# One plain fp32 matmul in place of three rounded ones in the mixers of a two-layer diffusion backbone

## What is computed

```python
hc = ctx * (1 + mods_c[1]) + mods_c[0]
proj_c = hc @ (w_in[l][:, :SCAN_COLS] if last else w_in[l])
xh_c, b_c, c_c, dtf_c, dtb_c = ssd_prepare(proj_c[..., :SCAN_COLS], conv_w[l], conv_b[l])
...
h = x * (1 + sc1) + sh1
proj = h @ w_in[l]
...
merged = (jax.nn.sigmoid(proj[..., COL_GP:COL_GS]) * y_pool
          + jax.nn.sigmoid(proj[..., COL_GS:W_IN_COLS]) * y_s)   # y_s = normed y @ w_ssd_out
return merged @ w_o
...
x = layer_norm(DEEPNORM_ALPHA * x + g1 * mix, ln_g[l, 0], ln_b[l, 0])
```

## Time and profile before

| | us |
|---|---|
| median of 3 runs | 4869.28 (4862.14 to 4878.07) |
| the profiled execution (its span) | 4879.2 |
| context projection, at 44 to 161 | 117 |
| context merge, at 269 to 413 | 144 |
| latent finish, at 1432 to 1556 | 124 |
| latent projection, at 2984 to 3151 | 167 |
| latent merge, at 3260 to 3508 | 248 |

### The profile page before, as it was taken

One profiled execution on the slowest core, in us unless ns is written; L12 is line 12 of the kernel. 1 busy time (PEld: TensorE's weight loads), 2 busy tenths in 40 slices (PEclk: granted clock), 3 DMA queues, 4 the chain that ended last, 5 costly groups with the idle time before them and its releaser, 6 DMA issues. The chain is left out here.

```text
span 4879.2 us, 47619 instructions
## 1 busy us (share of the span) xinstructions
PE 3455.5 (71%) x15218; PEld 1732.2 (36%) x15218; DVE 3203.2 (66%) x6594; ACT 1529.7 (31%) x3727; POOL 2178.8 (45%) x1603
## 2 busy tenths in 40 slices
PE   7788888987768987555555557979897555555555
PEld 5576323432357433111111115767742111111111
DVE  5365787664465668776776756674566677677775
ACT  2452344343262225222222223372222222222221
POOL 3253444443022454555555552323245555555554
PEclk9889999998879999767777778979999777777777
DMA  4536999999732999999999992232299999999998
GB/s 180 212 126 226 390 419 407 413 425 376 293 126 91 375 419 394 406 416 417 408 422 419 413 424 79 71 104 78 87 373 405 421 406 421 417 416 423 413 420 356
DMA packets 263605, 1596.67 MB, mean 327 GB/s; under 512 B 43885, under 2 KB 50861, under 8 KB 77357
## 3 DMA queue, kind: packets, MB, share of 16 engines
q0 software_dynamic: 184320, 1342.26, 66.5%
q1 hardware_dynamic: 77738, 248.58, 14.0%
q10 hardware_dynamic: 1296, 2.79, 0.2%
HBM read 1575.86 MB, written 17.66 MB: 327 GB/s over the span
## 5 line engine op out<-in xcount | busy, mean ns | idle before, releaser
L2465 PE MATMUL banks<-arena 128*64 128x512 f32 x5120 | 1596.4, 761 | 1106.6 <-ACT arena L2288 1102.8
L2072 POOL DMA_INDIRECT arena<-in_experts,arena x1280 | 1524.1, 1191 | 1615.7 <-PE banks L2465 1350.6
L2158 DVE CUSTOM_DVE_ANT_0 arena<-arena,token_copies 128x1024 f32<-128x1024 f32 x1280 | 1625.5, 1288 | 686.0 <-DMA arena<-in_experts,arena 618.9
L2465 PEld LDWEIGHTS banks<-arena 128*64 128x64 f32 x5120 | 387.0, 167 | 2154.1 <-ACT arena L2288 1517.0
L2281 ACT ACTIVATE arena<-arena 128x2 f32<-128x2 f32 x640 | 131.2, 205 | 1768.3 <-DVE arena L2158 1754.8
L286 POOL TENSOR_TENSOR wide_low<-wide_blocks,wide_high 128x1024 fp32r<-128x1024 f32 x136 | 340.6, 2526 | 594.9 <-ACT wide_high L276 594.9
L2288 ACT ACTIVATE arena<-arena 128x64 f32<-128x64 f32 x1280 | 376.2, 340 | 293.3 <-POOL arena L1943 251.9
L2344 PE MATMUL banks<-arena,wide_blocks 128*128 128x512 f32 (+3 forms) x960 | 311.5, 474 | 8.4 <-ACT arena L2187 6.7
L324 PE MATMUL banks<-activation_a,wide_high 128*128 128x512 f32 (+1 forms) x768 | 277.8, 362 | 8.5 <-ACT arena L348 2.7
L2417 PE MATMUL banks<-arena,wide_blocks 128*128 128x512 f32 x576 | 276.9, 618 | 0.0
L326 PE MATMUL banks<-activation_a,wide_low 128*128 128x512 f32 (+1 forms) x768 | 269.2, 351 | 0.0
(11 more groups left out here) (256 smaller groups left out, 4679.3 us busy)
## 6 DMA issues: line engine op xcount, KB each, us to landing
wide_blocks<-in_wide SPq DMA_DIRECT2D x168, 1024.0 KB
arena<-cum_rows SPq DMA_DIRECT2D x80, 256.0 KB, 3.2
arena<-in_experts,arena POOLq DMA_INDIRECT x1280
pre_scan<-arena SPq DMA_DIRECT2D x16, 256.0 KB
arena<-pre_scan SPq DMA_DIRECT2D x16, 256.0 KB, 9.1
residual<-in_tokens SPq DMA_DIRECT2D x6, 512.0 KB
arena<-mod_rows SPq DMA_DIRECT2D x6, 512.0 KB
norm_rows<-in_keys SPq DMA_DIRECT2D x3, 1024.0 KB
```

The lines of the kernel that those rows point to most:

```text
L2072: pool.indirect_dma_start(out=v.ring[:, g % RING], out_offset=None, in_=io["experts"], in_offset=bass.IndirectOffsetOnAxis(ap=c.idx[:, u % ...
L2158: last = nc.vector.tensor_tensor_reduce(out=u_row, in0=u_row, in1=k.copies[:, n % NJ], scale=1.0, scalar=0.0, op0=ALU.mult, op1=ALU.add, a ...
L2465: mm = nc.tensor.matmul(k.ps[j * QUAD:(j + 1) * QUAD, a + half], v.lhs[:, g % 4, j], v.ring[:, (g * NJ + j) % RING, D + half * BANK:D + (h ...
```

## The change

In the five stages `product` does one fp32 matmul per pair of tiles, on the weight block as it landed and on the activation as fp32. The splitting goes on all engines: `round_wides`, `cut_wides`, `take_wide` and `modulate_rest` are gone, the second writing of modulated tiles, the second half of the dt matmuls, and the splits of y and of the merged sum. TensorE waits for a block's landing in place of its split. In `stage_project` the turned tiles are copied by ScalarE instead of VectorE, and the scan products rotate over four banks instead of two. In `stage_merge` the pooling products move to banks 2 and 3.

```diff
-def round_wides(k, act, last):
-    while k.next_round <= last:
...
-        for rows in HALVES:
-            k.nc.scalar.copy(k.wide_hi[:, n % HI_SLOTS, rows], k.wide[:, n % WIDE_SLOTS, rows]) \
-                .then_inc(k.wide_rounded.sem, 1)
...
-def cut_wides(k, pool, last):
...
-            k.nc.gpsimd.tensor_tensor(k.wide_lo[:, n % WIDE_SLOTS, rows], k.wide[:, n % WIDE_SLOTS, rows],
-                                      k.wide_hi[:, n % HI_SLOTS, rows].bitcast(F32), ALU.subtract) \
-                .then_inc(k.wide_cut.sem, 1)
...
+def wait_wide(k, pe, n):
+
+    pe.wait_ge(k.wide_landed[n % WIDE_SLOTS].sem, 16 * (n // WIDE_SLOTS + 1))
...
 def product(k, pe, out, lhs, rhs, ready=None):
...
-        if kt == KT // 2 and k.second_half:
-            pe.wait_ge(k.wide_cut.sem, k.second_half)
-            k.second_half = 0
-        (lh, ll), (rh, rl) = lhs(kt), rhs(kt)
-        signal_used(k, nc.tensor.matmul(out, lh, rh, start=(kt == 0), stop=False))
-        nc.tensor.matmul(out, lh, rl, start=False, stop=False)
-        last = nc.tensor.matmul(out, ll, rh, start=False, stop=(kt == KT - 1))
+        last = k.nc.tensor.matmul(out, lhs(kt), rhs(kt), start=(kt == 0), stop=(kt == KT - 1))
+        if kt == 0:
+            signal_used(k, last)
...
-        if kt >= 2:
-            act.wait_ge(k.h_ready.sem, k.h_ready.at(kt - 1))
-        for dst, sig in ((k.act_a[:, kt, 0:T], None), (v.hraw[:, kt % 2, 0:T], k.h_hi)):
...
+        k.nc.scalar.activation(k.act_h[:, kt, 0:T], k.ps[:, kt % 2, 0:T], ACT.Identity,
+                               bias=v.modc[:, 0, kt:kt + 1], scale=v.modc[:, 1, kt:kt + 1]).then_inc(k.h_ready.sem, 1)
...
-            for n in range(2 * KT):
-                kt, q = n % KT, n % 4
...
+            for kt in range(KT):
+                q = kt % 4
...
+            def copy_turned(act, m):
+
+                act.wait_ge(k.turned.sem, k.turned.at(m + 1))
...
+                if 3 <= m < 3 + X_TILES + B_TILES:
+                    copy_turned(act, m - 3)
```

The stages' own lines change in the same way, for instance in the output products of `stage_merge` and `stage_finish`:

```diff
+                if n == 1:
+                    pe.wait_ge(k.merged1.sem, k.merged1.at(KT))
                 if n >= 4:
                     pe.wait_ge(k.mix_read.sem, k.mix_read.at(n - 3))
 
                 product(k, pe, k.ps[:, n % 4, 0:WIDE], lambda kt: mT(kt, slice(t * P, (t + 1) * P)),
-                        lambda kt: tuple(part[:, kt] for part in w),
-                        ready=(lambda kt: pe.wait_ge(k.merged_lo.sem, k.merged_lo.at(kt + 1))) if n == 0 else None) \
+                        lambda kt: w[:, kt],
+                        ready=(lambda kt: pe.wait_ge(k.merged1.sem, k.merged1.at(kt + 1))) if n == 0 else None) \
```

More of the change, by code:

```diff
@@ L28 @@
 U32 = mybir.dt.uint32
-F32R = mybir.dt.float32r
 ALU = mybir.AluOpType
@@ L113, in sb, with alias @@
         return nc.alloc_sbuf_tensor_at(name, shape, dt, offset=k.place[name])
-    def alias(name, shape, other, words=0, dt=F32R):
+    def alias(name, shape, other, words=0, dt=F32):
         return nc.alloc_sbuf_tensor_at(name, shape, dt, offset=k.place[other] + 4 * words)
@@ L120, in setup @@
     k.wide = sb("wide_blocks", [P, WIDE_SLOTS, KT, WIDE])
[L121 to L126, removed]
+    k.copies = sb("token_copies", [P, NJ, D])
+    k.rows = sb("norm_rows", [P, 2, D])
+    k.gates = alias("pooled_gates", [P, 8, SEQ], "token_copies")
     k.ident = sb("identity", [P, P])
@@ L138, in setup @@
     split = lambda name, at: alias(name, [P, KT, SEQ], "arena", at)[:]
[L139 to L143, removed]
+    k.act_h = split("modulated", A_HT)
+    k.act_y = split("gated_outputs", A_XTOK)
     k.ps = ctx.enter_context(nc.psum_tensor("banks", [P, 8, BANK], F32))
@@ L505, in more_mods @@
         x.advance(16 * rounds)
-    k.cut0, k.next_round, k.next_cut = k.cut0 + count, k.next_round + count, k.next_cut + count
     return m
@@ L545, in stage_project @@
     n_wide = 12 if full else 8
-    last_cut = n_wide - 1 if layer == 0 else n_wide
-    hT = lambda kt, cut=slice(0, T): (k.act_a[:, kt, cut], k.act_d[:, kt, cut])
+    hT = lambda kt, cut=slice(0, T): k.act_h[:, kt, cut]
     ld = k.loaded.base
@@ L600, in _ @@
             pe.wait_ge(k.loaded.sem, ld + 48)
-            for n in range(2 * KT):
-                kt, q = n % KT, n % 4
-                last = nc.tensor.matmul(k.ps[32 * q:32 * q + 32, 6, 0:T], v.wdt[:, kt], hT(kt)[n // KT].bitcast(F32),
-                                        start=(n < 4), stop=(n >= 2 * KT - 4))
+            for kt in range(KT):
+                q = kt % 4
+                last = nc.tensor.matmul(k.ps[32 * q:32 * q + 32, 6, 0:T], v.wdt[:, kt], hT(kt),
+                                        start=(kt < 4), stop=(kt >= 4))
             last.then_inc(k.dt_parts.sem, 1)
             for n in range(zg):
-                wh, wl = take_wide(k, pe, w0 + 8 + n // NT)
-                if n == 2:
-                    pe.wait_ge(k.padded.sem, k.padded.at(SCAN_TILES))
+                w = k.wide[:, (w0 + 8 + n // NT) % WIDE_SLOTS]
+                t = n % NT
+                if t == 0:
+                    wait_wide(k, pe, w0 + 8 + n // NT)
+                if n < 2:
+                    pe.wait_ge(k.padded.sem, k.padded.at(SCAN_TILES - 1 + n))
                 if n >= 4:
                     pe.wait_ge(k.z_done.sem, k.z_done.at(n - 3))
-                t = n % NT
                 product(k, pe, k.ps[:, n % 4, 0:WIDE], lambda kt: hT(kt, slice(t * P, (t + 1) * P)),
-                        lambda kt: (wh[:, kt], wl[:, kt])).then_inc(k.z_proj.sem, 1)
+                        lambda kt: w[:, kt]).then_inc(k.z_proj.sem, 1)
                 if n == 2:
@@ L651, in _ @@
             for n in range(zg):
-                if n % NT == 0 and n >= NT:
-                    round_wides(k, act, w0 + min(8 + n // NT + 1, last_cut))
                 act.wait_ge(k.z_proj.sem, k.z_proj.at(n + 1))
@@ L664, in _ @@
                     decay.decays(act)
-        @block.gpsimd
-        def _(pool):
-            cut_wides(k, pool, w0 + last_cut)
         @block.vector
@@ L709, in stage_project @@
     k.consts_set.advance(2)
-    for s in (k.xt_ready, k.h_hi, k.h_ready):
+    for s in (k.xt_ready, k.h_ready):
         s.advance(KT)
@@ L1781, in stage_finish @@
     k.rms_ready.advance(1)
-    for x in (k.ys_proj, k.merged1, k.yt_turned, k.yt_copied, k.y_hi, k.merged_hi, k.merged_lo):
+    for x in (k.ys_proj, k.merged1, k.yt_turned, k.yt_copied):
         x.advance(8)
```

188 lines of the change are left out of this document (51 added, 137 removed).

## The result

The changed kernel takes 4917.1 us at the median (4911.4 to 4922.9, 4 runs), the kernel before 4868.2 in the same session (4862.1 to 4878.1, 4 runs). The ratio is 1.0097, with a 95% interval of 1.0079 to 1.0114: slower by 1.0%, 49 us. Forecast was +74, 4943, in a range from 4910 to 4985. The time lies in the range, close to its lower end, and the +49 just under the "slower by 50 to 100 us" that had been given 0.80. The sign and the mechanism held; of the forecast 74 us a third did not come.

The account below looks back on a forecast made before the run. TensorE was taken to set four of five stages, VectorE, held up by GpSimd's splitting, the context projection. Stage nets 37 + 26 + 13 + 10 - 12 gave +74 (141 growth, 67 returned) on 4869.28: 4943, range 4910 to 4985.

Parts of the forecast that it names:

- growth: Five stages: longer plain fp32 products on TensorE's path add 141 us, 17 of it in the context projection.
- relief: Five stages: splitting work and waits that go away return 67 us, uncertain by 20 either way.
- The price, 512 columns: Eight-step product in the stages: two records of 0.430 us per plain matmul, 6.88 us against 5.57, +1.31.
- The rival built on the ratio 4/3, 4994: Five stages: four passes against three make products a third longer, 192 us less 67, +125; chance 0.05.
- The price, 256 columns: Eight-step product in the stages: two records of 0.224 us per plain matmul, 3.58 us against 2.87, +0.71.
- Tails: Ends of latent merge and latent finish: 1.6 and 1.9 us added, in the merge because the fourth layer norm comes late.
- about 3 us in all: Latent merge start: turned tiles written once save a ScalarE pass each, but four transposes then set the pace.
- a rival in the wrong direction: Six kinds of section: one more product each at 1.2 GHz, twice as long, 41 us more, 4984; chance 0.04.
- The context projection: TensorE becomes the bound, 3.58 us a product; the stage ends at 149 instead of 161, net -12, the only gain.
- what would show it: Right: 2560 product records, sigmoids 6.9 us apart, taps 2.16 us, no TensorE wait for VectorE, latent merge about 285 us.
- the signs of being wrong: Fewer or closer records, shorter stages outside the context projection, granted clock under 1.00 in dense stretches, or waits for weight blocks.

Follow-up runs that it names:

- price-alone kernel: Kernel before with one plain fp32 matmul per product step instead of three split ones, all splitting work and waits kept: 4978.2 us, ratio 1.0221.

## Why the prediction was nearly right

By stage, in us: growth and relief as forecast, and as measured (growth is the price-alone kernel less the kernel before, relief the changed kernel less the price-alone kernel).

| stage | forecast growth, relief, net | measured growth, relief, net |
|---|---|---|
| latent merge | 46, -9, +37 | 44.7, -15.6, +29.0 |
| latent projection | 32, -6, +26 | 29.0, -6.5, +22.6 |
| latent finish | 20, -7, +13 | 17.0, -7.8, +9.1 |
| context merge | 25, -15, +10 | 17.6, -14.1, +3.5 |
| context projection | 17, -29, -12 | 0.1, -14.0, -13.9 |
| sum | 141, -67, +74 | 108.3, -58.0, +50.3 |

**The price, 512 columns.** +1.31 forecast, 6.86 - 5.57 = +1.29 measured. Right, and with it the reading that a plain matmul leaves two records. A product's time grew by a factor of 1.23, not 4/3: a split matmul takes 0.23 us, more than a quarter of a plain one's 0.86. The rival built on the ratio 4/3, 4994, is out. By the Trainium skill ("FP8 and Floating Point Precision", section "TensorE Precision Notes") true FP32 takes four passes; counted against three single ones they do not give the time here.

**The price, 256 columns.** This is the term that was mis-sized. I took 0.224 a record, "nearer the middle of its bounds"; it is 3.46 / 16 = 0.216, half of 512's as the lower bound had it. The growth is 0.59 and not 0.71 a product. That is 0.12 for each of 73 products outside the context projection, 9 us. The lower bound was half of the measured price for 512; the upper one, 3.72 / 16, held the last matmul's tail, which a dense run pays once and not sixteen times. The middle between them had no claim.

**Tails.** I added 1.6 and 1.9 us at the ends of the latent merge and finish. In the merge the read of the product that completes the first row tile stands at 3515.71 and the last operation ends at 3540.42: 24.7 us, where it had been 24.3. TensorE's later products let the first three norms move under them, and the fourth was no later.

```profile
3515.71 0.42 DVE L1267 TENSOR_TENSOR arena<-banks,arena 128x256 f32<-128x256 f32 x1 [2.16 <-PE banks L277]
...
3539.14 1.28 DVE L1023 SCALAR_TENSOR_TENSOR residual<-residual,arena 128x1024 f32<-128x1024 f32 x1
```

With 1.29 and 0.59 the four stages outside the context projection would grow by 110 us (52 products of 512 and 73 of 256), and they grew by 108.3. Two of them differ from it by more than their spread. The latent merge grew by 44.7 and not 42.6: the price-alone kernel's first product takes 10.2 us at a granted clock of 0.69, that of the kernel before 7.2 at 0.85, so that it costs 3.0 more where a product at full clock costs 1.29. The context merge grew by 17.6 and not 20.7: TensorE waited there four times, 2.6 us in all, for the rest of a split block from GpSimd (L286), and in the price-alone kernel, where products are longer, not once.

**Relief.** Right in three stages to within a microsecond, though in the latent projection its spread of 4.0 between profiles is larger than that. In the latent merge I had 9 and it is 15.6: at the start I counted a ScalarE pass a tile with the transposes next in line, "about 3 us in all", and it is 8.5. Of that, 5.4 are the turning, and 3.1 the first product, which had not been counted at all: it now starts at full clock. Nearly 2 of the 3.1 only undo the extra growth named above; against the kernel before, the first product is done 5.5 us earlier (19.7 and 14.2). I had seen that the latent stages start at the lower level and used it only for a rival in the wrong direction.

**The context projection.** TensorE did become the bound, at 3.67 us a tile, and the stage ends 103 us after its start (100 and 101 in the two profiles without the fall of the clock); I had 105. Growth and relief do not add up here: taken first, the price costs nothing, since VectorE sets the scan (117.0 and 117.1), and the relief without the price is 26.3. With both, the price costs 12.4 (90.8 to 103.2, or 9.5 with the stage at 100.3), where 24 x 0.59 = 14 would be the whole of it. That GpSimd held up VectorE is shown twice, by taking its work away and by putting it back.

Of the 24 us between +74 and +50, 15 are growth outside this stage (9 the 256-column price, 3 the tails, 3 the waits in the context merge), 6 relief (the latent merge's start), 2 this stage.

**What stood under "what would show it".** The 2560 records of `product`, 16 between two sigmoids that stand 6.9 us apart (6.86), taps of 2.16 and no wait of TensorE for VectorE in the scan came as written; the latent merge is 277 and not 285 long; the three lookups are as long as before within 4 us. Of the signs of being wrong one did appear in small: the granted clock is under 1.00 in two dense stretches, 0.83 at the end of the context projection (1.7 us) and 0.91 from 3120 to 3140 in the latent projection. The kernel before has 0.91 in the same place of its latent projection (3114 to 3134), so at least that one is no effect of plain matmuls.

## What to carry to other kernels

Price an instruction that a trace does not show by counting how many records a known one leaves, and take its pace from start to start in a dense run; if the run's bounds are apart, look for a better known price to divide: here half of the 512-column record gave 0.215 and the measured one was 0.216, while the middle of the bounds was 4% off. A change that makes the busiest engine slower and its helpers freer is several changes: decide it stage by stage, by who sets the pace there. Here the one stage in which VectorE did is the only one worth changing, and that version is faster than either kernel. And work on GpSimd is not free because nobody waits for it: ask what VectorE does beside it.

## What the runs showed of the hardware

Two things I had not expected in their size. One GpSimd subtraction of 128 x 1024 fp32 values (2.4 to 2.6 us) that runs beside VectorE's fp32 taps costs VectorE 1.93 us, nearly its own length; 24 of them, with 1.9 us in which TensorE itself waited for their results, made a stage 26 us longer in which VectorE set the pace, and 34 of them changed nothing in the latent merge, where TensorE does. And a second ScalarE pass of 0.67 us a tile between the transposes of two tiles at a stage's start lowers TensorE's granted clock there from 0.62 to 0.50, and that of the 9.8 us behind it from 1.00 to 0.85, so that the first product takes 8.5 us and not 7.1. Such falls also came without any edit: the same 48 matmul records at the end of the context projection took 10.61 us in three profiles (1.00) and 12.29 in three others (0.83).
